# A two-layer streaming encoder on one core: the attention's order on VectorE, ScalarE and TensorE, and who scales the identity

## The chip, the cores and the metric

The kernel runs on one core of one Trainium2 chip. The metric is the device time of one execution in microseconds (us). A core has a matrix engine (TensorE, PE in the profile, with its weight loads as PEld), VectorE (DVE), ScalarE (ACT), GpSimd (POOL) and a queue engine that starts transfers (SyncE, SP). Each engine takes its instructions strictly in the order in which the program has them. They meet at semaphores alone.

## The reference

Two layers over 576 tokens (512 of a prompt in chunks of 64, 64 of a sample with 512 past ones), in fp32:

```
h = x + 1/2 SwiGLU_1(rms(x))
a = rms(h) @ w_in                     # split into three groups of heads
  A  latent attention, 6 heads: scores over the whole past, softmax, values from a 128-wide latent
  B  banded attention, 6 heads: 3 chunks of keys, a learned sink, a bias of slope * distance
  C  gated linear recurrence, 4 heads, then RMSNorm(o) * silu(g)
h = h + concat(A, B, C) @ w_out
h = h + 1/2 SwiGLU_2(rms(h))
h = h + sigmoid(rms(h) @ ple_gate) * (p @ ple_proj)
```

## The kernel before

It is written by hand: every engine has its own program, and the order of its lines is the order of the work. A loop runs over the two layers. In a layer the dense products (`dense`) take each weight tile as a high and a low half, three products each; before and after the attention they keep TensorE full. Between the last of them in `mixer_inputs` (`swq2`) and the first of the output projection (`out0`) stands `attention`, with no dense work beside it. This case is about that stretch.

**Units.** `attention` goes through 30 units: 6 pairs of heads times 5 variants v. v = 0 to 3 are the four blocks of 128 prompt queries, v = 4 is the sample. Pairs 0 to 2 (units 0 to 14) are the banded ones ("swa"): 128, 256, 256, 256 and 192 keys. Pairs 3 to 5 (units 15 to 29) are the latent ones ("mla"): 128, 256, 384, 512 and 576 keys. Before each latent pair `project` makes its keys, queries and values in six pieces, R, K, N, E, C, V.

**One unit through the engines.** TensorE makes the scores (`scores`) in one of two score slots in PSUM. VectorE adds the bias and the sink in banded units, takes the row maximum and scales it (`bound`). ScalarE takes the exponential and its row sum (`softmax_exp`). VectorE inverts the sum (`invert`). GpSimd multiplies the identity matrix by it (`scale_identity`, `scaled_id`). TensorE turns the probabilities with this scaled identity (`turn`), into one PSUM area (banks 6 and 7), so `turn` of a unit waits until ScalarE has copied the one before (`copy_t`). Then `weigh` multiplies by the values, into banks 4 and 5.

**The order before**, in iteration u, is: TensorE `scores(u+3)`, `turn(u+1)`, `weigh(u)` (turn first where a projection or the mean squares follow). ScalarE `copy_t(u+1)`, `softmax_exp(u+3)`. VectorE `invert(u+2)`, `bound(u+3)`. When a pair is through, `outputs` splits its 576 columns into `hid_hi` (ScalarE) and `hid_lo` (VectorE), and `weigh` of the next pair's unit with v = 0 waits for that, since it writes the same banks.

**The recurrence's tail** is worked off inside the attention: `head_out` copies its last result (`H1`), a Square makes `tmp`, `mean_squares` sums it on TensorE at u = `MEAN_SQUARES`, ScalarE takes a Sqrt, and `head_norm` on VectorE runs, behind `bound`, two reciprocals of 128x576, a scaling, a product and a subtraction at the units in `HEAD_NORM` and at `HEAD_HI` + 1. `take` copies the last level of the recurrence (`L13`), and `H1` on TensorE waits for it.

Of the kernel before, what the change touches and what calls it, by code (L numbers as in the profile page):

```python
# [23 lines left out]
F32 = mybir.dt.float32  # L24
# [6 lines left out]
P = 128  # L31
# [99 lines left out]
MEAN_SQUARES, HEAD_NORM, HEAD_HI = 8, (15, 16, 18, 19), 21  # L131
# [65 lines left out]
def hybrid_step(nc, x_t, p_t, w_all, uq, ukv, par_d, logits_d, cos_sin, ident_d, ones_d, head_ones_d, comb_d,  # L197
# [3 lines left out]
    with ctx:  # L201
# [68 lines left out]
        tmp = place("tmp", [P, 2, TOK], at=hid_at)  # L270
# [48 lines left out]
        def hg_bank(name):  # L319

            return 4 + 2 * (STEPS.index(name) % 2)
# [87 lines left out]
        att_hi = ev("att_hi", PAIRS)  # L409
        att_lo = ev("att_lo", PAIRS)  # L410
# [9 lines left out]

        out_flat = ps[:, 4:6, :].rearrange("p a n -> p (a n)")[:, 0:TOK]
# [95 lines left out]
        def _(act):  # L517
# [80 lines left out]
            def mixer_inputs(L):  # L598
# [37 lines left out]
                head_out(L, 1)  # L636
                act.wait_ge(O_out.sem, O_out.at(L, 4))
                act.activation(tmp[:, 0:2, :], hk[:, :, :], ACT.Square).then_inc(O_sq.sem, 1)
# [88 lines left out]
            def outputs(L, pair):  # L727

                act.wait_ge(pv_done.sem, pv_done.at(L, VARIANTS * (pair + 1)))
                if pair == 3:  # L730
                    act.wait_ge(O_norm.sem, O_norm.at(L, 3))
                act.activation(hid_hi[:, out_tile(pair), :], out_flat, ACT.Copy).then_inc(att_hi.sem, 1)

            def attention(L):
                softmax_exp(L, 0)
                softmax_exp(L, 1)
                copy_t(L, 0)
                softmax_exp(L, 2)
                for u in range(UNITS):
                    if u and u % VARIANTS == 0:  # L740
                        outputs(L, u // VARIANTS - 1)
# [15 lines left out]
                outputs(L, PAIRS - 1)  # L757
# [29 lines left out]
        def _(dve):  # L787
# [159 lines left out]
            def mixer_inputs(L):  # L947
                for name in W_IN:
# [42 lines left out]
                    elif name == "swk":  # L991
# [12 lines left out]
                        for j in range(2):  # L1004
                            dve.scalar_tensor_tensor(cq[:, j, :], cq[:, j, :],
                                                     par[:, PAR["q_norm"] + j:PAR["q_norm"] + j + 1],
                                                     c_root[:, :], ALU.mult, ALU.mult).then_inc(c_norm.sem, 1)
                    else:
                        scaled(L, u, halves(swq[:, int(name[3]), :])).then_inc(drained.sem, 1)
                dve.tensor_scalar(sink8[:, :], par[:, PAR["sink"]:PAR["sink"] + 6], 1 / SWA_SCALE, None, ALU.mult) \  # L1010
                   .then_inc(c_norm.sem, 1)
                take(L, 2 * LEVELS - 1)
# [125 lines left out]

            def bound(L, u):

                kind, pr, v = unit(u)
                b, x, nk = u % 2, X["s", u], unit_keys(u)
                made_wait(dve, L, x)
                if kind == "swa":
                    for a in range(2):
                        rows = slice(64 * a, 64 * a + 64) if v == 4 else slice(0, P)
                        at = 0 if v == 4 else a
                        hd = pr + 3 * a
                        if v == 4:
                            k0 = 64 * a  # L1150
                            dve.tensor_copy(score[rows, b, 0, nk:nk + 1], sink8[rows, hd:hd + 1])
                        else:
                            k0 = 128 if v == 0 else 0
                            if a == 0:
                                dve.tensor_copy(score[:, b, :, nk], sink8[:, pr:6:3])
                        slope = 2.0 ** (-8.0 * (hd + 1) / 6)
                        dve.scalar_tensor_tensor(score[rows, b, at, 0:nk], dist[rows, k0:k0 + nk],
                                                 -slope / SWA_SCALE, s_pair(x)[rows, a, 0:nk],
                                                 ALU.mult, ALU.add).then_inc(s_free[x % 2].sem, 1)
                    slot_wait(dve, L, x)  # L1160
                    n, src = (1, score[:, b, 0, 0:nk + 1]) if v == 4 else (2, score[:, b, :, 0:nk + 1])
                elif v == 4:
                    n, src = 1, s_flat(x)[:, 0:nk]
                else:
                    n, src = 2, s_pair(x)[:, :, 0:nk]
# [5 lines left out]
            def invert(L, u):  # L1171
# [5 lines left out]
                dve.reciprocal(stat[:, b, 6:6 + n], stat[:, b, 4:4 + n]).then_inc(recip_done.sem, 1)  # L1177

            def outputs(L, pair):

                dve.wait_ge(att_hi.sem, att_hi.at(L, pair + 1))
                dve.tensor_tensor(hid_lo[:, out_tile(pair), :], out_flat,
                                  hid_hi[:, out_tile(pair), :].bitcast(F32), ALU.subtract).then_inc(att_lo.sem, 1)

            def attention(L):
                dve.wait_ge(c_norm.sem, c_norm.at(L, 5))
                bound(L, 0)
                bound(L, 1)
                invert(L, 0)
                invert(L, 1)  # L1190
# [11 lines left out]
                outputs(L, PAIRS - 1)  # L1202
# [51 lines left out]
        def _(pool):  # L1254
# [37 lines left out]
            with pool.Fori(0, DEPTH) as L:  # L1292
# [17 lines left out]
                for u in range(UNITS):  # L1310
# [8 lines left out]
        def _(pe):  # L1319
# [291 lines left out]
            def turn(L, u):  # L1611
# [3 lines left out]
                if u == 0:  # L1615
# [257 lines left out]
```

## Time and profile before

| | us |
|---|---|
| median of 3 runs (2555.94 to 2561.65) | 2558.96 |
| the profiled execution | 2559.2 |
| its span | 2557.4 |
| attention of layer 1, 600.19 to 737.73 | 137.54 |
| attention of layer 2, 1856.77 to 1994.07 | 137.30 |

In the profile, "idle before" is the time in which the engine waited just ahead of an instruction, with the engine and line that ended it. PEclk is the share of full speed that TensorE was granted: 1.0 is 2.4 GHz, 0.5 is 1.2 GHz. A timeline row merges equal instructions ("x8").

### The profile page before, as it was taken

The page shows a single profiled execution, that of the slowest core. Times are in us where ns is not written, and L with a number is a line of the kernel's source. Part 1 is how long each engine was busy: PE and PEld are TensorE (multiplying, and loading weights), DVE is VectorE, ACT ScalarE, POOL GpSimd, SP SyncE. Part 2 cuts the span into 40 slices and gives each one's busy share as a digit, 9 for nine tenths or more (in the row PEclk, how much of TensorE's full clock was granted, in tenths as well). Part 3 has the DMA queues.
Part 4 walks back from the last instruction along what each step waited for, and adds up shares of the span by engine and source line. Part 5 has one row for each costly group of instructions (what it writes and reads, how often), then busy time and mean ns, then how long its engine had stood idle before and what let it go on. Part 6 is the DMA issues. An engine that isn't in the chain of part 4 may idle for free. (4 is left out here: it accounts for less than half of the span.)

```text
span 2557.4 us, 48070 instructions
## 1 busy us (share of the span) xinstructions
PE 2459.9 (96%) x19186; PEld 2384.1 (93%) x19186; DVE 1233.3 (48%) x1613; ACT 773.0 (30%) x1111; POOL 297.8 (12%) x211
## 2 busy tenths in 40 slices
PE   5999999998899999999999999999989999999996
PEld 5999999987689999999999999999857999999996
DVE  6434334775535434335654343458645354343466
ACT  3212223433543212223232221235245332221232
POOL 3000003101122000004300000040011400000043
PEclk9999999998999999999999999999989999999998
DMA  3322222211012222222223222232110222222222
GB/s 131 113 85 79 86 79 94 85 57 47 1 34 83 82 83 82 83 83 99 83 68 120 74 82 90 74 99 75 51 30 1 67 78 87 77 82 82 82 90 87
DMA packets 58569, 196.00 MB, mean 77 GB/s; under 512 B 8944, under 2 KB 11248, under 8 KB 58296
## 3 DMA queue, kind: packets, MB, share of 16 engines
q1 hardware_dynamic: 56848, 190.70, 22.7%
q10 hardware_dynamic: 1584, 3.37, 0.4%
q8 instruction: 98, 1.61, 0.3%
q14 instruction: 39, 0.32, 0.0%
HBM read 190.16 MB, written 3.88 MB: 76 GB/s over the span
## 5 line engine op out<-in xcount | busy, mean ns | idle before, releaser
L1343 PE MATMUL ps<-xg_hi,w_hi 128*128 128x288 f32 x3616 | 780.4, 297 | 32.4 <-DVE w_lo L796 28.3
L1343 PE MATMUL ps<-xg_lo,w_hi 128*128 128x288 f32 x3616 | 775.5, 296 | 0.0
L1343 PE MATMUL ps<-xg_hi,w_lo 128*128 128x288 f32 x3616 | 775.4, 296 | 0.0
L1343 PEld LDWEIGHTS ps<-xg_hi,w_hi 128*128 128x128 f32 x3616 | 584.2, 189 | 35.3 <-issue 28.3
L1343 PEld LDWEIGHTS ps<-xg_lo,w_hi 128*128 128x128 f32 x3616 | 584.2, 189 | 0.0
L1343 PEld LDWEIGHTS ps<-xg_hi,w_lo 128*128 128x128 f32 x3616 | 584.0, 189 | 0.0
L796 DVE TENSOR_TENSOR w_lo<-w_raw,w_hi 128x1024 fp32r<-128x1024 f32 x347 | 437.3, 1261 | 242.1 <-ACT w_hi L534 237.7
L534 ACT ACTIVATE w_hi<-w_raw 128x1024 fp32r<-128x1024 f32 x347 | 364.0, 1050 | 424.1 <-PE ps L1343 410.9
L1343 PE MATMUL ps<-hid_hi,w_hi 128*128 128x288 f32 x1664 | 356.6, 296 | 0.0
L1343 PE MATMUL ps<-hid_lo,w_hi 128*128 128x288 f32 x1664 | 356.2, 296 | 0.0
L1343 PE MATMUL ps<-hid_hi,w_lo 128*128 128x288 f32 x1664 | 356.2, 296 | 0.0
L1343 PEld LDWEIGHTS ps<-hid_hi,w_hi 128*128 128x128 f32 x1664 | 268.2, 189 | 0.1
L1343 PEld LDWEIGHTS ps<-hid_lo,w_hi 128*128 128x128 f32 x1664 | 268.2, 189 | 0.0
L1343 PEld LDWEIGHTS ps<-hid_hi,w_lo 128*128 128x128 f32 x1664 | 268.2, 189 | 0.0
L890 DVE SCALAR_TENSOR_TENSOR h<-ps,h 128x576 f32 (+1 forms) x96 | 72.7, 758 | 278.7 <-PE ps L1343 278.3
L575 ACT ACTIVATE hid_hi<-val 128x576 f32 (+1 forms) x88 | 60.3, 686 | 479.7 <-DVE val L871 479.7
L1258 POOL TENSOR_TENSOR acc<-h 128x576 f32<-128x576 f32 x9 | 12.0, 1333 | 1619.4 <-DVE h L890 1546.7
L816 DVE TENSOR_TENSOR val<-ps,r 128x576 f32<-128x576 f32 x88 | 66.6, 757 | 217.4 <-PE ps L1343 217.4
L816 DVE TENSOR_TENSOR gate<-ps,r 128x576 f32<-128x576 f32 x104 | 78.7, 757 | 174.0 <-PE ps L1343 172.4
L571 ACT ACTIVATE gate<-gate 128x576 f32<-128x576 f32 x88 | 60.4, 686 | 334.9 <-DVE gate L816 334.9
L1263 POOL TENSOR_TENSOR acc<-acc,sq 128x576 f32<-128x576 f32 x63 | 133.7, 2122 | 4.9
L1261 POOL TENSOR_TENSOR sq<-h 128x576 f32<-128x576 f32 x63 | 104.2, 1654 | 115.1 <-DVE h L1240 46.5
(208 smaller groups left out, 1669.8 us busy)
## 6 DMA issues: line engine op xcount, KB each, us to landing
w_raw<-w_all SPq DMA_DIRECT2D x347, 512.0 KB, 3.4
h<-x_t ACTq DMA_DIRECT2D x1, 2304.0 KB, 9.6
y_t<-y SPq DMA_DIRECT2D x8, 288.0 KB, 2.2
uq_w<-uq SPq DMA_DIRECT2D x2, 768.0 KB, 4.9
p_raw<-p_t SPq DMA_DIRECT2D x2, 576.0 KB, 7.0
ukv_w<-ukv SPq DMA_DIRECT2D x2, 384.0 KB
ckv<-ckv_c SPq DMA_DIRECT2D x2, 256.0 KB, 5.4
ckv_o<-ckv SPq DMA_DIRECT2D x2, 256.0 KB, 2.1
```

What stands on the lines that cost most here:

```text
L534: act.activation(w_hi[:, s, :], w_raw[:, n % RAW_SLOTS, :], ACT.Copy).then_inc(whi_ready.sem, 1)
L571: act.activation(gate[:, pr, :], gate[:, pr, :], ACT.Silu).then_inc(silu_done.sem, 1)
L575: act.activation(hid_hi[:, tile + pr + i * 2, :], val[:, pr, :], ACT.Copy) \
L796: dve.tensor_tensor(w_lo[:, s, :], w_raw[:, n % RAW_SLOTS, :], w_hi[:, s, :].bitcast(F32), ALU.subtract).then_inc(wlo_ready.sem, 1)
L816: return dve.tensor_tensor(out, slot(u), halves(r[:, :]), ALU.mult)
L890: dve.scalar_tensor_tensor(halves(h[:, m, :]), slot(v0 + q), 0.5, halves(h[:, m, :]), ALU.mult, ALU.add).then_inc(drained.sem, 1)
L1258: pool.tensor_tensor(acc[:, :], h[:, 0, :], h[:, 0, :], ALU.mult).then_inc(acc_done.sem, 1)
L1261: pool.tensor_tensor(sq[:, :], h[:, t, :], h[:, t, :], ALU.mult).then_inc(sq_done.sem, 1)
L1263: pool.tensor_tensor(acc[:, :], acc[:, :], sq[:, :], ALU.add).then_inc(acc_done.sem, 1)
L1343: ins = pe.matmul(ps[:, bank(u) + c, 0:HALF], w, m[:, k, c * HALF:(c + 1) * HALF], start=(k == kts[0] and i == 0), stop=(k == kts[-1] and ...
```

## The change

Six things change in one edit, all inside the attention or at its start.

1. VectorE's `bound` is cut in two. `bias` (sink and distance of a banded unit) goes ahead of `invert`, and `bound` keeps the maximum.
2. In latent units VectorE writes `scaled_id` itself, inside `invert`, ahead of the next maximum. GpSimd scales the identity in units 0 to 14 only.
3. `outputs` of a pair is in two parts, the 512 prompt columns and the 64 sample columns. `weigh` waits for part 0 at v = 0 and for part 1 at v = 4. On VectorE the parts stand behind `bound` of iterations 5p+5 and 5p+6 (p is the pair) where one subtraction stood ahead of `invert`.
4. ScalarE's last `head_out` goes behind the first two exponentials, and the Square behind that of unit 3. `H1` writes banks 4 and 5 where it wrote 6 and 7, so `weigh(0)` waits for `head_out` and `turn(0)` doesn't.
5. `take` of level 13 goes ahead of the weight split of the "spare" chunk, and the scaling of the sinks into `swk`'s work.
6. The mean squares move from u = 8 to 17, the two reciprocals from u = 15 and 16 to 18 and 19, the rest from 18, 19, 21 to 21, 22, 23, and `tmp` to another place in memory.

The constants, the bank of the recurrence's products, and ScalarE's `attention`:

```diff
-MEAN_SQUARES, HEAD_NORM, HEAD_HI = 8, (15, 16, 18, 19), 21
+MEAN_SQUARES, HEAD_NORM, HEAD_HI = 17, (18, 19, 21, 22), 23
...
-            return 4 + 2 * (STEPS.index(name) % 2)
+            return 6 - 2 * (STEPS.index(name) % 2)
...
             def attention(L):
                 softmax_exp(L, 0)
                 softmax_exp(L, 1)
                 copy_t(L, 0)
+                head_out(L, 1)
                 softmax_exp(L, 2)
                 for u in range(UNITS):
-                    if u and u % VARIANTS == 0:
-                        outputs(L, u // VARIANTS - 1)
...
+                    if u % VARIANTS == 4:
+                        outputs(L, u // VARIANTS, 0)
+                    if u and u % VARIANTS == 0:
+                        outputs(L, u // VARIANTS - 1, 1)
+                    if u == 0:
+                        act.wait_ge(O_out.sem, O_out.at(L, 4))
+                        act.activation(tmp[:, 0:2, :], hk[:, :, :], ACT.Square).then_inc(O_sq.sem, 1)
```

VectorE's `invert` (its last lines) and `attention`, then TensorE's `weigh`:

```diff
                 dve.reciprocal(stat[:, b, 6:6 + n], stat[:, b, 4:4 + n]).then_inc(recip_done.sem, 1)
+                if unit(u)[0] == "mla":
+                    dve.wait_ge(recip_done.sem, recip_done.at(L, u + 1))
+                    dve.wait_ge(id_ready.sem, id_ready.at(L, u))
+                    dve.wait_ge(turned.sem, turned.at(L, u - 1))
+                    for a in range(n):
+                        ins = dve.tensor_scalar(scaled_id[:, b, a, :], ident[:, :], stat[:, b, 6 + a:7 + a], None,
+                                                ALU.mult)
+                    ins.then_inc(id_ready.sem, 1)
...
                 for u in range(UNITS):
-                    if u and u % VARIANTS == 0:
-                        outputs(L, u // VARIANTS - 1)
                     if opens_mla_pair(u + 3):
                         project(L, unit(u + 3)[1])
+                    if u + 3 < UNITS and unit(u + 3)[0] == "swa":
+                        bias(L, u + 3)
                     if u + 2 < UNITS:
                         invert(L, u + 2)
                     if u + 3 < UNITS:
                         bound(L, u + 3)
+                    if u >= VARIANTS and u % VARIANTS in (0, 1):
+                        outputs(L, u // VARIANTS - 1, u % VARIANTS)
                     head_norm(L, u)
...
-                if v == 0 and u:
-
-                    pe.wait_ge(att_lo.sem, att_lo.at(L, u // VARIANTS))
+                if u == 0:
+                    pe.wait_ge(O_out.sem, O_out.at(L, 4))
+                if v in (0, 4) and u >= VARIANTS:
+
+                    pe.wait_ge(att_lo.sem, att_lo.at(L, 2 * (u // VARIANTS) - (1 if v == 0 else 0)))
```

First place: VectorE in a full banded unit. Before, iteration 0: `invert` (the reciprocal of `stat`), the sink's copy, the bias from `dist`, the maximum and its scaling.

```order
L428 REGISTER_ALU
L1177 RECIPROCAL stat_120<-stat_120 128x2
L1155 COPY score_85<-sink8_75 128x2
L1157 SCALAR_TENSOR_TENSOR score_85<-dist_66,ps 128x256 x2
L1166 TENSOR_REDUCE stat_120<-score_85 128x2
L1167 REGISTER_ALU
L1168 TENSOR_SCALAR stat_120<-stat_120 128x2
```

The changed kernel, the same iteration:

```order
L1158 COPY score_85<-sink8_75 128x2
L1160 SCALAR_TENSOR_TENSOR score_85<-dist_66,ps 128x256 x2
L429 REGISTER_ALU
L1186 RECIPROCAL stat_120<-stat_120 128x2
L1175 TENSOR_REDUCE stat_120<-score_85 128x2
L1176 REGISTER_ALU
L1177 TENSOR_SCALAR stat_120<-stat_120 128x2
```

The copy and the bias moved from behind the reciprocal, which waits for an exponential, to ahead of it.

Second place: VectorE around the two reciprocals of `tmp`. Before, they stand in iterations 15 and 16, and the next rows are piece R of the projection that iteration 17 opens.

```order
L1110 RECIPROCAL tmp_98<-tmp_98 128x576
L434 REGISTER_ALU
L1177 RECIPROCAL stat_120<-stat_120 128x2
L1166 TENSOR_REDUCE stat_120<-ps 128x1
L1167 REGISTER_ALU
L1168 TENSOR_SCALAR stat_120<-stat_120 128x1
L1110 RECIPROCAL tmp_98<-tmp_98 128x576
L438 REGISTER_ALU
L1128 TENSOR_TENSOR tq_99<-ps,cs_61 128x576
```

The changed kernel, from the maximum of unit 22 (iteration 19) to the subtraction of pair 3's prompt part (iteration 20):

```order
L1175 TENSOR_REDUCE stat_120<-ps 128x2
L1176 REGISTER_ALU
L1177 TENSOR_SCALAR stat_120<-stat_120 128x2
L1114 RECIPROCAL tmp_98<-tmp_98 128x576
L435 REGISTER_ALU
L1186 RECIPROCAL stat_120<-stat_120 128x2
L1192 TENSOR_SCALAR scaled_id_119<-ident_62,stat_120 128x128 x2
L1175 TENSOR_REDUCE stat_120<-ps 128x2
L1176 REGISTER_ALU
L1177 TENSOR_SCALAR stat_120<-stat_120 128x2
L1200 TENSOR_TENSOR hid_lo_53<-ps,hid_hi_52 128x512
```

The second reciprocal moved from in front of a projection to between two units of one pair, and the subtraction of the finished pair stands behind it and behind the maximum of unit 23.

Third place: ScalarE at the start of the attention. Before (`hk` is `head_out`, `tmp` the Square, `prob` the exponentials):

```order
L663 ACTIVATE hk_78<-ps 128x256
L663 ACTIVATE hk_78<-ps 128x320
L637 ISA
L638 ACTIVATE tmp_98<-hk_78 128x1152
L692 ISA
L699 ACTIVATE prob_117,stat_120<-score_85,stat_120 128x129 x2
```

The changed kernel:

```order
L697 ACTIVATE prob_117,stat_120<-score_85,stat_120 128x129 x2
L690 REGISTER_ALU
L697 ACTIVATE prob_117,stat_120<-score_85,stat_120 128x257 x2
L722 ACTIVATE probT_118<-ps 128x2x128
L661 ACTIVATE hk_78<-ps 128x256
L661 ACTIVATE hk_78<-ps 128x320
```

Two exponentials and a copy moved ahead of `head_out`; the Square moved further down.

## Rows read from the trace of the kernel before

**Rows 1.** The page: engines, busy time, share of the span, instructions.

```profile
PE 2459.9 (96%) x19186; PEld 2384.1 (93%) x19186; DVE 1233.3 (48%) x1613; ACT 773.0 (30%) x1111; POOL 297.8 (12%) x211
```

**Rows 2.** By stage: us, then busy us of PE, PEld, DVE, ACT, POOL, then PEclk.

```profile
600.19:654.42 54.23, 41.99 (x348) 30.53 (x349) 29.06 (x99) 27.76 (x79) 10.41 (x16) 0.81 0.12 36
654.42:737.73 83.31, 78.61 (x564) 59.97 (x562) 40.05 (x66) 42.03 (x100) 8.95 (x16) 0.98 0.00 1
1856.77:1912.43 55.66, 43.19 (x349) 31.96 (x349) 29.06 (x99) 27.99 (x79) 10.40 (x16) 0.79 0.12 35
```

**Rows 3.** TensorE and its granted clock (PEclk), in two short stretches.

```profile
632.00:636.00 4.00, 4.00 (x25) 0.57 0.00 0
...
680.00:684.00 4.00, 4.00 (x14) 0.57 0.00 0
...
1936.00:1940.00 4.00, 3.36 (x23) 1.00 0.02 4
```

**Rows 4.** Timeline of layer 1, start of attention (start, duration, engine, instruction, wait).

```profile
601.16 2.26 POOL L1307 COPY kT<-krs 32x1024 f32<-32x1024 f32 x2 [74.90 <-DVE swq L816]
...
601.31 1.96 DVE L796 TENSOR_TENSOR w_lo<-w_raw,w_hi 128x1024 fp32r<-128x1024 f32 x1 [0.33 <-ACT w_hi L534]
...
604.34 0.35 PE L1525 MATMUL ps<-A,V 64*64 64x64 f32 x5 [1.65 <-DVE A L1100]
...
609.57 1.16 ACT L638 ACTIVATE tmp<-hk 128x1152 f32<-128x1152 f32 x1
...
612.54 1.19 PE L1629 MATMUL ps<-scaled_id,prob 128*128 128x128 f32 x4 [2.60 <-POOL scaled_id L1284]
```

**Rows 5.** Timeline, one round of the banded units and the turn of unit 6.

```profile
615.53 0.17 DVE L1177 RECIPROCAL stat<-stat 128x2 f32<-128x2 f32 x1 [1.16 <-ACT prob L699]
...
616.44 0.69 DVE L1166 TENSOR_REDUCE stat<-score 128x2 f32<-128x514 f32 x1
...
618.53 0.17 DVE L1177 RECIPROCAL stat<-stat 128x2 f32<-128x2 f32 x1 [1.20 <-ACT prob L699]
...
627.13 1.13 PE L1629 MATMUL ps<-scaled_id,prob 128*128 128x128 f32 x8 [0.60 <-POOL scaled_id L1284]
```

**Rows 6.** Timeline, TensorE in front of `weigh` of unit 5.

```profile
630.54 0.44 PE L1653 MATMUL ps<-probT,swv 128*64 128x128 f32 x4 [2.28 <-DVE hid_lo L1182]
```

**Rows 7.** Timeline, the mean squares of unit 8 and the turn of unit 10.

```profile
638.95 1.28 ACT L748 ACT_TABLE_LOAD   x1 [0.78 <-PE ps L1538]
640.25 1.37 ACT L748 ACTIVATE tmp<-ps,eps 128x576 f32<-128x576 f32 x2
...
642.99 0.71 PE L1629 MATMUL ps<-scaled_id,prob 128*128 128x128 f32 x4
```

**Rows 8.** Timeline, the first long reciprocal, the turn of unit 18, then piece R.

```profile
674.02 3.75 DVE L1110 RECIPROCAL tmp<-tmp 128x576 f32<-128x576 f32 x1
...
678.63 2.49 PE L1629 MATMUL ps<-scaled_id,prob 128*128 128x128 f32 x16 [2.21 <-POOL scaled_id L1284]
...
680.92 3.35 PE L1558 MATMUL ps<-cq,uq_w 128*128 128x288 f32 x8
```

**Rows 9.** Timeline around unit 20: its exponential, turn of unit 21, `weigh` of unit 20.

```profile
692.94 0.37 ACT L705 ACTIVATE prob<-ps,stat 128x128 f32<-128x128 f32 x1
...
700.85 1.06 PE L1629 MATMUL ps<-scaled_id,prob 128*128 128x128 f32 x8
...
701.83 0.44 PE L1653 MATMUL ps<-probT,mv 128*64 128x128 f32 x4
```

**Rows 10.** VectorE groups by form: busy us, mean ns, idle before.

```profile
L1110 DVE RECIPROCAL tmp<-tmp 128x576 f32<-128x576 f32 x4 | 15.0, 3744 | 0.0
L1182 DVE TENSOR_TENSOR hid_lo<-ps,hid_hi 128x576 fp32r<-128x576 f32 x12 | 9.1, 757 | 28.2 <-ACT hid_hi L732 28.2
...
L1166 DVE TENSOR_REDUCE stat<-ps 128x2 f32<-128x1024 f32 x6 | 7.2, 1203 | 0.0
```

**Rows 11.** The page, the groups: the weight split of VectorE.

```profile
L796 DVE TENSOR_TENSOR w_lo<-w_raw,w_hi 128x1024 fp32r<-128x1024 f32 x347 | 437.3, 1261 | 242.1 <-ACT w_hi L534 237.7
```

More of the change, by code:

```diff
@@ L725, in copy_t, with outputs @@
                        .then_inc(probT_ready.sem, 1)
[L727 to L732, printed above, removed]
+            def outputs(L, pair, part):
+                cols = out_cols[part]
+                act.wait_ge(pv_done.sem, pv_done.at(L, VARIANTS * pair + 4 + part))
+                act.activation(hid_hi[:, out_tile(pair), cols], out_flat[:, cols], ACT.Copy).then_inc(att_hi.sem, 1)
             def attention(L):
@@ L1137, in project, with bias @@
                    .then_inc(s_free[dve_c % 2].sem, 1)
-            def bound(L, u):
-                kind, pr, v = unit(u)
+            def bias(L, u):
+                _, pr, v = unit(u)
                 b, x, nk = u % 2, X["s", u], unit_keys(u)
                 made_wait(dve, L, x)
-                if kind == "swa":
[L1145 to L1159, printed above, removed]
@@ new lines, in bias @@
+                for a in range(2):
+                    rows = slice(64 * a, 64 * a + 64) if v == 4 else slice(0, P)
+                    at = 0 if v == 4 else a
+                    hd = pr + 3 * a
+                    if v == 4:
+                        k0 = 64 * a
+                        dve.tensor_copy(score[rows, b, 0, nk:nk + 1], sink8[rows, hd:hd + 1])
+                    else:
+                        k0 = 128 if v == 0 else 0
+                        if a == 0:
+                            dve.tensor_copy(score[:, b, :, nk], sink8[:, pr:6:3])
+                    slope = 2.0 ** (-8.0 * (hd + 1) / 6)
+                    dve.scalar_tensor_tensor(score[rows, b, at, 0:nk], dist[rows, k0:k0 + nk],
+                                             -slope / SWA_SCALE, s_pair(x)[rows, a, 0:nk],
+                                             ALU.mult, ALU.add).then_inc(s_free[x % 2].sem, 1)
@@ L1177, in invert, with outputs @@
                 dve.reciprocal(stat[:, b, 6:6 + n], stat[:, b, 4:4 + n]).then_inc(recip_done.sem, 1)
[L1179 to L1183, printed above, removed]
+                if unit(u)[0] == "mla":
[6 more added lines that the diff above has]
+                    ins.then_inc(id_ready.sem, 1)
+            def outputs(L, pair, part):
+                cols = out_cols[part]
+                dve.wait_ge(att_hi.sem, att_hi.at(L, 2 * pair + part + 1))
+                dve.tensor_tensor(hid_lo[:, out_tile(pair), cols], out_flat[:, cols],
+                                  hid_hi[:, out_tile(pair), cols].bitcast(F32), ALU.subtract) \
+                   .then_inc(att_lo.sem, 1)
             def attention(L):
                 dve.wait_ge(c_norm.sem, c_norm.at(L, 5))
-                bound(L, 0)
-                bound(L, 1)
+                for u in range(2):
+                    bias(L, u)
+                    bound(L, u)
                 invert(L, 0)
+                bias(L, 2)
                 invert(L, 1)
@@ L1309, in _ @@
                         .then_inc(k_placed.sem, 1)
-                for u in range(UNITS):
+                for u in range(UNITS // 2):
                     scale_identity(L, u)
```

39 lines of the change are left out of this document (20 added, 19 removed).

## The prediction

> **What bounds the kernel now.** The page comes first: TensorE is busy for 96% of the span [rows 1], so only its idle time and the time at half clock can be won. The busy table by stage says where they are. The attention of layer 1 takes 137.5 us. In its banded part TensorE works 42.0 of 54.2 us at a mean clock of 0.81, in its latent part 78.6 of 83.3 us at 0.98; in layer 2 the banded part takes 55.7 [rows 2]. So the banded part is bound by waiting, with 12 us idle in each layer, and the latent part by TensorE itself: there each new wait of TensorE is lost in full. The dense stages are not touched. The timeline then says what TensorE waits for, and I follow it unit by unit. "T(u)", "S(u)" and "W(u)" are TensorE's `turn`, `scores` and `weigh` of unit u.
>
> **The gain in the banded part.** I shift the landmarks T(0), T(6), T(10) and the first projection, in layer 1.
>
> *The start.* T(0) runs at 612.54. It waits for an identity whose exponential stands behind `head_out` and a Square of 1.16 us, and `H1` itself waited 1.65 us for `take` behind a weight split of 1.96 us [rows 4]. Changed, `take` runs first and the exponential right after its maximum. VectorE still works off the split, two biases and two maxima, which ended near 607 before; the first reciprocal comes then, and GpSimd's identity 0.9 us later. T(0) at about 608.3, gain 4.2.
>
> *The round.* VectorE and ScalarE alternate: reciprocal at 615.53, next one at 618.53, 3.0 us a unit. From the first reciprocal to the maximum at 616.44 lie 0.91 us, and some 0.83 of them are copy and bias, which now run while ScalarE is at the previous exponential; the round falls to about 2.15 us. TensorE's own work for a full unit is a turn of 1.13 [rows 5], scores of about 0.6 and `weigh` of about 0.6, 2.3 us in all. So a full unit costs about 2.3, not 3.0. In pair 0 this is used up: `head_out` (0.7) and the Square (1.16) now stand among its exponentials. T(6), at 627.13, comes at about 623.35, gain 3.8.
>
> *The pair's end.* W(5) waited 2.28 us for `hid_lo` [rows 6]. In the new order W(5) waits for a subtraction behind `bound(8)`, which needs S(8), which TensorE issues only one turn ahead of W(5). From the end of S(8): bias 0.85, reciprocal and maximum with its scaling 1.1, subtraction 0.7, handovers 0.2, sum 2.85; TensorE has 1.1 of work. It idles about 1.75 us, so this part wins only 0.5 of each stop.
>
> *The mean squares leave.* At u = 8 they cost TensorE 2.1 us of products (8 of 288 columns, as piece R) and ScalarE a table load of 1.28 and 1.37 of Sqrt ahead of T(10) at 642.99, and the load stands again behind the Sqrt, for the next exponential [rows 7]. Without them a light unit is left there, about 2 us. T(10) at 633.85, gain 9.1, 4.1 of it from the mean squares. Pair 2 is shorter by three rounds of 0.7: the projection starts at 643.2, against 654.42 [rows 2]. **Gain 11.2 us**, and 12.6 in layer 2, whose banded part is 1.4 longer now at the same work [rows 2].
>
> **The losses in the latent part.**
>
> *W(15).* Before, the subtraction stood ahead of `invert` and W(15) waited little. Now it stands behind `bound(18)`, whose maximum over 1024 columns takes 1.20 [rows 10], and VectorE has also scaled two identities in each round. No row shows such a scaling of 128 columns. It is bounded by an instruction of two columns, 0.17 [rows 5], and by the subtraction of 576 columns, 0.76 [rows 10], whose share for 128 would be 0.17 as well; I take 0.35 for two of them, with 0.35 to 1.5 as ends (the two ends are the two rows taken as they stand; 1.5 would add 3.5 us to the chain of W(20) below). From the end of S(18): 0.1 + 0.6 (reciprocal, identities) + 1.2 + 0.2 + 0.7 + 0.1 = 2.9, against a turn of 1.06. Loss 1.85.
>
> *T(18).* It waited 2.21 us, since a reciprocal of 3.75 us stood ahead of its own [rows 8]. That wait is gone, which pays for W(15) and the identities: T(18) stays at 678.6.
>
> *Mean squares.* They now stand behind T(18): 2.1 us on TensorE, then piece R needs a slot that the table load and the first Sqrt free, 1.2 later: loss 3.3. In layer 1 T(18) took 2.49 and R 3.35 at half clock (0.57 over that stretch); at full clock they would take about 2.0 and 2.1, as in layer 2, where the clock stayed at 1.0 [rows 3, 8]. That is 1.7 back in layer 1. Together with rounding, the end of R is 1.85 later in layer 1 and 3.5 in layer 2.
>
> *W(20), the largest term.* The exponential of unit 20 started at 692.94 [rows 9]; the table load to come back from Sqrt now stands ahead of it, 1.28, so 694.2. On VectorE, one after the other: `invert(20)` from 695.05, with identities 0.6, `bound(21)` 0.9, **reciprocal 3.74**, `invert(21)` 0.6, `bound(22)` 1.15 (between the 0.69 of 512 columns and the 1.20 of 1024), **reciprocal 3.74** [rows 5, 10], `invert(22)` 0.6, `bound(23)` 1.4, subtraction 0.7, handover 0.1. That is 13.5 from 695.05, so 708.5, and W(20) before was at 701.83, directly behind T(21) [rows 9]. TensorE has nothing else it may issue. Loss 6.7. Behind W(20) stand S(24), T(22), W(21) and T(23); they follow at their own pace.
>
> *W(25).* As W(15), with the last subtraction of `head_norm` ahead, twice as wide as the 0.76 row: W(25) can go 1.45 later than before. Loss 1.45.
>
> *The clock.* After T(18)'s wait the granted clock fell to 0.57 in the mean of 4 us in layer 1, between the levels of 1.2 and 2.4 GHz, and stayed at 1.0 after the same wait in layer 2 [rows 3, 8]. A low stretch under full load costs about 1.6. I count one behind W(20) and one more, 1.5, for the five shorter waits of 1.2 to 1.85 us in a layer.
>
> **The sum.** Layer 1: 11.2 - 1.85 - 6.7 - 1.45 - 1.6 - 1.5 = -1.9. Layer 2: 12.6 - 3.5 - 6.7 - 1.45 - 1.6 - 1.5 = -2.15. That is 4.0 us slower than 2559.2, the profiled execution, which lies 0.2 above the median of 2558.96: 2563.2. A gain of the first half is taken away by the second.
>
> **A rule beside a row.** The weight split at 601.31 took 1.96 us, against 1.26 in the mean of its kind [rows 11], while GpSimd copied `kT` from 601.16 to 603.42 [rows 4]. The Trainium skill, GPSIMD Engine Reference, section 1 (Specifications), says that GpSimd's way to SBUF is shared with VectorE and that VectorE instructions with two SBUF inputs contend with it; the split has two, and the trace agrees. By that rule `take` loses nothing by going first, and the split, moved behind it, shortens by the part that then lies behind GpSimd's copy, about 0.5 us a layer; by the row alone it stays at 1.96. The sum above keeps 1.96; by the rule it would be 1 us better, 2562.2.
>
> **The rivals.**
>
> *A, the forecast:* the two halves nearly cancel, within 5 us of before. 0.43.
>
> *B, slower:* each of the shorter waits brings the half clock, as the wait of 2.21 us in layer 1 did [rows 3, 8]. Three more low stretches a layer at 1.5, less where TensorE waits anyway, give 3 to 4.5 a layer: 2570 to 2572. Half of it already decides, from 2564.1 on. For it: the idle time gets new places in the latent part, where TensorE is 94% busy now. Against it: the waits are shorter than that one, and after the same wait in layer 2 the clock stayed. 0.39.
>
> *C, faster:* the start no longer has the two waits of 1.65 and 2.60 us [rows 4], and the clock doesn't fall there at all. In the banded part, whose mean was 0.81 [rows 2], most of the low clock lies there. Then pair 0 runs 1 to 1.5 us faster, and with no low stretch but that behind W(20) a layer gains 2.5 to 3 over the sum: 2557.7. It decides (2553.8) only if the W(20) chain is also 2 us shorter than I have it, or the banded rounds reach 2.15 us in place of 2.3 (11 of them, 1.6 us a layer). 0.18.
>
> *D, the bias ahead of `invert` brings nothing,* since it has to wait for S(u+3) and then holds `invert(u+2)`. For it: same queue, in order. Against it: TensorE issues S(u+3) a full turn ahead. At 0.83 for nine full units it would be 7.5 us in each layer, 2578. It is in B's chance, as less than 0.03.
>
> About 0.2% is what a measurement of this kernel can tell from no change, here 5.1 us. Faster 0.18, same 0.43, slower 0.39. The range, 2552 to 2572, takes in B to its upper end and C to about its middle; the forecast's own is 2554 to 2564.
>
> **What would show it.** In the changed profile: T(0) near 608.3; reciprocals of `stat` 2.2 to 2.5 us apart in full banded units; the banded part, 600.2 to the first piece R, near 43 us in place of 54.2; in front of `weigh` of unit 20 an idle time of 6 to 7 us on TensorE put down to `hid_lo`; two table loads around the second projection; the latent part near 96 us in place of 83.3. Wrong would make it: a W(20) that follows T(21) at once, or low clock in other places than I have put it.

## The result and the profile after

The changed kernel takes 2555.52 us in the median of 20 runs (2551.26 to 2560.58), the one before 2559.58 in as many beside it. The medians lie 4.1 us apart. The ratio of the two sets is 0.9986, with an interval from 0.9980 to 0.9993, which is 3.6 us faster (1.8 to 5.1), where 4.2 slower was forecast. The gain is real and about as small as this measurement can tell. The profiled span is 2553.8 against 2557.4.

The busy table by stage of the changed kernel (us; busy of PE, PEld, DVE, ACT, POOL; PEclk; DMA share; GB/s): banded and latent part of layer 1, then of layer 2.

```profile
599.97:640.22 40.25, 33.40 (x342) 24.66 (x341) 27.73 (x100) 23.50 (x77) 9.41 (x16) 0.96 0.17 48
640.22:735.13 94.91, 81.83 (x573) 61.85 (x571) 47.08 (x97) 46.67 (x108) 0.40 (x1) 0.96 0.00 1
1853.68:1895.45 41.77, 34.90 (x341) 25.99 (x341) 27.73 (x100) 23.43 (x77) 9.41 (x16) 0.92 0.16 46
1895.45:1990.44 94.99, 82.21 (x572) 62.14 (x571) 47.08 (x97) 46.66 (x108) 0.40 (x1) 0.95 0.00 1
```

Against [rows 2] the banded part lost 14.0 and 13.9 us (forecast 11.2 and 12.6), and the latent part became 11.6 and 13.3 longer (forecast 13.1 and 14.75). So layer 1 is 2.4 faster and layer 2 0.5; the other 0.7 of the span is small shifts outside the attention. The forecast was right that two large amounts nearly cancel, and wrong about which is larger.

Timeline of the start of layer 1, where [rows 4] stood: GpSimd's copy, the split, `H1`, and the turn of unit 0.

```profile
600.95 1.26 POOL L1331 COPY kT<-krs 32x1024 f32<-32x1024 f32 x2 [74.94 <-DVE swq L819]
...
602.54 1.21 DVE L799 TENSOR_TENSOR w_lo<-w_raw,w_hi 128x1024 fp32r<-128x1024 f32 x1
...
602.79 0.35 PE L1549 MATMUL ps<-A,V 64*64 64x64 f32 x5 [0.32 <-DVE A L1104]
...
607.47 0.68 PE L1651 MATMUL ps<-scaled_id,prob 128*128 128x128 f32 x4 [1.17 <-POOL scaled_id L1308]
```

T(0) comes at 607.47 (forecast 608.3). The split takes 1.21 in place of 1.96 and GpSimd's copy 1.26 in place of 2.26: they no longer lie side by side, and the split is as short as the mean of its kind [rows 11]. T(0)'s four matmuls end in 0.68 us, not 1.19, since the clock is up. The next view is TensorE's granted clock over the first 20 us of the attention, layer 1 and 2, first of the kernel before and then of the changed one.

```profile
600.18:620.18 20.00, 15.45 (x159) 0.66 0.31 95
1856.77:1876.77 20.00, 15.46 (x159) 0.66 0.33 95
```

```profile
599.97:619.97 20.00, 17.10 (x213) 1.00 0.33 96
1853.68:1873.68 20.00, 17.10 (x213) 1.00 0.33 96
```

In the same time TensorE does 213 matmuls in place of 159. Further on in layer 1 the timeline has W(5), W(10) and the first piece R. [rows 6] had 2.28 us of waiting at W(5). Behind W(10) the clock still falls (0.66 in the mean of 635 to 640 us):

```profile
623.03 0.44 PE L1677 MATMUL ps<-probT,swv 128*64 128x128 f32 x4 [1.71 <-DVE hid_lo L1200]
...
635.15 0.44 PE L1677 MATMUL ps<-probT,swv 128*64 128x128 f32 x4 [1.71 <-DVE hid_lo L1200]
...
640.22 2.11 PE L1582 MATMUL ps<-cq,uq_w 128*128 128x288 f32 x8
```

And the latent part, layer 1: W(15), the table load and R(1), then the chain ahead of W(20), and W(25).

```profile
660.21 0.44 PE L1677 MATMUL ps<-probT,mv 128*64 128x128 f32 x4 [1.71 <-DVE hid_lo L1200]
...
667.22 1.28 ACT L744 ACT_TABLE_LOAD   x1
...
669.31 2.21 PE L1582 MATMUL ps<-cq,uq_w 128*128 128x288 f32 x8 [1.23 <-ACT tmp L744]
...
683.73 3.75 DVE L1114 RECIPROCAL tmp<-tmp 128x576 f32<-128x576 f32 x1
...
687.54 0.48 DVE L1192 TENSOR_SCALAR scaled_id<-ident,stat 128x128 f32<-128x128 f32 x2
...
689.00 3.75 DVE L1114 RECIPROCAL tmp<-tmp 128x576 f32<-128x576 f32 x1
...
693.20 1.22 DVE L1175 TENSOR_REDUCE stat<-ps 128x2 f32<-128x1024 f32 x1
...
694.53 0.68 DVE L1200 TENSOR_TENSOR hid_lo<-ps,hid_hi 128x512 fp32r<-128x512 f32 x1
...
695.36 0.69 PE L1677 MATMUL ps<-probT,mv 128*64 128x128 f32 x4 [6.06 <-DVE hid_lo L1200]
...
724.63 0.44 PE L1677 MATMUL ps<-probT,mv 128*64 128x128 f32 x4 [1.31 <-DVE hid_lo L1200]
```

Every stop of the forecast is there: 1.71 at W(15) (1.84 from its chain), 1.23 at R(1) (1.2), 6.06 at W(20) (6.7), 1.31 at W(25) (1.45). W(20)'s four matmuls take 0.69 in place of 0.44, since the clock is at half around the long stop (0.50 in the mean of 693.8 to 700.5 us).

### The profile page after: what moved, and what is told of

The parts are those of the page before. It is cut to its first block and busy times, and to the rows that moved or that the text cites. A ratio compares the mean times of both kernels' runs of the same rounds, so it can differ in the third digit from the quotient of the medians.

```text
span 2553.8 us, 48090 instructions
## 1 busy us (share of the span) xinstructions
PE 2450.7 (96%) x19186; PEld 2376.8 (93%) x19186; DVE 1244.0 (49%) x1679; ACT 772.3 (30%) x1123; POOL 278.7 (11%) x181
```

## The experiments

All twelve are edits of the changed kernel. Medians, and ratios to the kernel before on the same chip; stages in us, layer 1 / layer 2, from the one profiled execution. Kernels from different chips are compared by the ratio.

| kernel | median | ratio | span | banded | latent |
|---|---|---|---|---|---|
| before | 2559.58 | | 2557.4 | 54.2 / 55.7 | 83.3 / 81.6 |
| changed | 2555.52 | 0.9986 (0.9980 to 0.9993) | 2553.8 | 40.2 / 41.8 | 94.9 / 95.0 |
| E1 second reciprocal later | 2554.11 | 0.9981 (0.9971 to 0.9990) | 2548.5 | 40.2 / 41.8 | 91.9 / 92.5 |
| E2 GpSimd scales all | 2554.36 | 0.9976 (0.9966 to 0.9985) | 2548.6 | 40.2 / 41.8 | 92.1 / 92.4 |
| E3 bias behind `invert` | 2575.06 | 1.0062 (1.0045 to 1.0079) | 2573.6 | 49.2 / 49.2 | 95.0 / 95.0 |
| E4 old start | 2567.78 | 1.0032 (1.0018 to 1.0046) | 2562.0 | 44.0 / 46.6 | 94.8 / 94.6 |
| E5 `outputs` ahead, latent | 2547.93 | 0.9948 (0.9932 to 0.9965) | 2546.5 | 40.2 / 40.4 | 90.6 / 90.1 |
| E6 = E1 + E2 | 2546.96 | 0.9945 (0.9928 to 0.9961) | 2548.4 | 41.7 / 41.8 | 90.0 / 90.9 |
| E7 = E1 + E2 + E5 | 2536.82 | 0.9912 (0.9896 to 0.9929) | 2529.4 | 40.2 / 39.1 | 85.0 / 85.0 |
| E8 mean squares at 8 | 2552.15 | 0.9973 (0.9962 to 0.9983) | 2552.4 | 44.8 / 45.1 | 90.2 / 89.8 |
| E9 = E7, `outputs` first everywhere | 2539.60 | 0.9927 (0.9910 to 0.9943) | 2536.3 | 42.2 / 44.0 | 85.0 / 85.0 |
| E10 = E9 + E8 | 2541.41 | 0.9931 (0.9914 to 0.9948) | 2538.7 | 48.4 / 46.7 | 80.6 / 80.6 |
| E11 = E7 + E8 | 2537.51 | 0.9918 (0.9902 to 0.9935) | 2530.9 | 43.6 / 43.6 | 80.6 / 80.6 |
| E12 = E7 again | 2537.75 | 0.9908 (0.9888 to 0.9928) | 2538.7 | 41.8 / 41.8 | 85.0 / 85.0 |

**E1, the second long reciprocal leaves W(20)'s chain.**

```diff
-MEAN_SQUARES, HEAD_NORM, HEAD_HI = 17, (18, 19, 21, 22), 23
+MEAN_SQUARES, HEAD_NORM, HEAD_HI = 17, (18, 21, 22, 23), 24
```

> The changed kernel with the second long reciprocal behind the maximum of unit 24 (iteration 21, in front of the third projection) in place of iteration 19, and the three steps after it one iteration later. Theory A (the wait of 6.06 us in front of weigh of unit 20 is the two reciprocals in one chain): that wait falls by 3.7 to about 2.3 us, the low clock behind it gets shorter or goes, the latent part falls from 94.9 to about 90 us in each layer, the span from 2553.8 to 2543 to 2547. Rival B (VectorE is simply full in the latent part, and wherever the reciprocal stands something waits for it): the wait appears in front of piece R of the third projection or a turn behind it, and the span stays within 2 us of 2553.8.

Its timeline ahead of W(20), layer 1:

```profile
690.17 0.57 ACT L703 ACTIVATE prob<-ps,stat 128x384 f32<-128x384 f32 x1
...
690.86 0.17 DVE L1186 RECIPROCAL stat<-stat 128x2 f32<-128x2 f32 x1 [1.30 <-ACT prob L703]
...
693.62 0.44 PE L1677 MATMUL ps<-probT,mv 128*64 128x128 f32 x4 [3.85 <-DVE hid_lo L1200]
```

The stop falls by 2.2 (expected 3.7), and no new one appears; the latent parts are 3.0 and 2.5 shorter (expected 4.9), and the span stays 1.5 above the expected 2543 to 2547. The reciprocal was worth 2.2 of its 3.75, mainly because once it is gone `invert(22)` waits 1.30 for the exponential of unit 22. That wait my expected 2.3 us had left out. The second reciprocal is a cause of the stop, but only down to the next arrival. What is shown is the length of the stop. In total time neither E1 nor E2 or E8 is told from the changed kernel: their intervals overlap with 0.9980 to 0.9993. The spans of E1 and E2, 5.3 and 5.2 below the changed kernel's, are each from the third shortest of ten executions.

**E2, who scales the identity.** VectorE's scaling in `invert` is taken out, and GpSimd's loop runs over `range(UNITS)` in place of `range(UNITS // 2)`.

> The changed kernel with GpSimd scaling the identity in all 30 units, as before. Theory A (in the latent part TensorE waits for VectorE's chain, and VectorE's own scaling lengthens it by 0.4 to 0.5 us a unit): the waits in front of weigh of units 15, 20 and 25 fall by 0.4, 1.3 and 0.4 us, the span falls by 2 to 4 us, to about 2551. Rival B (the turn waits for the scaled identity, so VectorE's shorter way to it, about 0.35 us, is what pays): turns of latent units wait for GpSimd and the span rises by 2 to 6 us. Rival C: neither is waited for, within 1 us.

W(15) waits 1.31 (from 1.71), W(20) 4.62 (from 6.06), W(25) 1.31 as before, and no turn waits for GpSimd. The 1.44 of W(20) is three pairs of scalings at the 0.48 that the rows above show, one in each `invert` of its chain. Letting VectorE scale the identity made the stops longer and shortened no other wait of the latent part.

**E3, the bias behind `invert` again.**

```diff
-                    if u + 3 < UNITS and unit(u + 3)[0] == "swa":
-                        bias(L, u + 3)
                     if u + 2 < UNITS:
                         invert(L, u + 2)
+                    if u + 3 < UNITS and unit(u + 3)[0] == "swa":
+                        bias(L, u + 3)
```

Ahead of the loop `bias(L, 2)` goes behind `invert(L, 1)` in the same way.

> The changed kernel with bias put back behind invert, so that a banded unit's bias waits for the exponential again. Theory A (the round of VectorE and ScalarE sets the pace of the banded part, and the 0.83 us of the bias is on it): full banded units go from about 2.3 to 3.0 us, the banded part grows by 5 to 7 us in each layer, the span to 2564 to 2568. Rival D (TensorE's own work sets the pace anyway): below 2 us a layer, span under 2558.

The banded part of layer 1, then W(5) in it:

```profile
603.05:652.30 49.25, 36.68 (x340) 26.98 (x341) 28.47 (x100) 23.77 (x77) 9.41 (x16) 0.86 0.14 39
```

```profile
629.89 0.69 PE L1677 MATMUL ps<-probT,swv 128*64 128x128 f32 x4 [3.42 <-DVE hid_lo L1200]
```

The banded parts grow by 9.0 and 7.4, more than the 5 to 7 expected. Of that 5.7 in either layer is idle time of TensorE (49.25 - 36.68 = 12.57 against 6.85, and 12.57 against 6.87), the rest low clock. W(5) and W(10) stop exactly twice as long, 3.42, and the turns wait up to 1.43. So the new place of the bias is the main step of the change. Another 3.1 of the 19.8 in the span come before the attention, where the edit touches nothing: low clock at the first matmuls and behind a wait near 538 us (below, E12).

**E4, the old start:** `head_out` and the Square ahead of the first exponentials, `take` of level 13 behind the split.

> The changed kernel with the start as before: the last head_out and the Square ahead of ScalarE's first exponentials, take of level 13 behind the weight split. Theory A (the waits at the start both cost their own length and bring the low clock from about 605 to 618, which costs more): the first turn comes 4 to 5 us later, the granted clock is at half for some 13 us again, the banded part grows by 5 to 7 us in each layer, the span to 2564 to 2568. Rival (the clock there doesn't follow the waits): the clock stays at 1.0 after 605 and a layer loses 2 to 4 us, because the Square leaves the rounds of pair 0, span 2558 to 2562.

The turn of unit 0 in layer 1 and in layer 2:

```profile
610.90 0.68 PE L1649 MATMUL ps<-scaled_id,prob 128*128 128x128 f32 x4 [3.12 <-POOL scaled_id L1306]
```

```profile
1870.07 1.19 PE L1649 MATMUL ps<-scaled_id,prob 128*128 128x128 f32 x4 [2.60 <-POOL scaled_id L1306]
```

The banded parts grow by 3.8 and 4.8, less than the 5 to 7 expected, and the span of 2562.0 lies at the rival's upper end; the rival's clock of 1.0 did not come. Over their first 20 us the clock is 0.91 in layer 1, where it falls just behind T(0), and 0.66 in layer 2, as before the change. In the changed kernel and in the eleven edits that keep its start, 24 stages in all, that mean is 1.00 each time. The low clock belongs to the old start.

**E5, the subtraction ahead of `invert`,** for u from 15 on; **E6,** E1 and E2 together; **E7,** all three.

```diff
+                    if u >= 15 and u % VARIANTS in (0, 1):
+                        outputs(L, u // VARIANTS - 1, u % VARIANTS)
                     if u + 2 < UNITS:
                         invert(L, u + 2)
...
-                    if u >= VARIANTS and u % VARIANTS in (0, 1):
+                    if VARIANTS <= u < 15 and u % VARIANTS in (0, 1):
```

> The changed kernel, but in the latent units (u from 15 on) VectorE's two `outputs` parts of a finished pair stand ahead of `invert` again, as before the change; the banded units stay as changed. Theory A: of the latent stops, W(15) 1.71, W(20) 6.06 and W(25) 1.31 us, the part that is spent in queue behind `invert` and `bound` comes back. W(15) and W(25) fall to under 0.5, W(20) loses an `invert` (0.6) and a `bound` (1.4) of its chain and goes to about 4.0; some 0.7 is given back where `invert` stands behind the subtraction. Span 2546 to 2549, against 2553.8 of the changed kernel. Rival: the subtraction delays the next identity by 0.7 each time and the stop moves to the turn behind it; the latent part keeps its 94.9 us and the span is 2552 to 2556.

> Both earlier edits at once: the second long reciprocal of `tmp` in iteration 21 in place of 19 (the rest at 22, 23, 24), and GpSimd scales the identity in all 30 units. Alone each took 5.3 and 5.2 us off the span of the changed kernel, 3.0 and 2.8 us of the latent part of layer 1. Theory A: both shorten the same chain in front of W(20), one after the other: W(20) idles 3.85 - 1.44 = 2.4 us, W(15) 1.31, W(25) 1.31, latent part near 89.1, span 2543 to 2545. Rival: another chain (exponential of 23 behind the table load) already stands behind the 3.85, so W(20) stays at 3.5 or more and the span at 2546 to 2549.

> The two edits on the reciprocals and on GpSimd, and in the latent units the `outputs` parts ahead of `invert`. Theory A: what VectorE queues in front of `hid_lo` is all there is in the latent stops, so all three are nearly gone: W(15) and W(25) under 0.5, W(20) about 1, latent part near 86.5 in place of 94.9 us, span 2537 to 2541, median about 2543. Rival: the turns now wait for GpSimd behind the subtraction, latent part 88.5 or more, span 2543 or more.

W(20) in E5, E6 and E7, layer 1:

```profile
695.53 0.69 PE L1679 MATMUL ps<-probT,mv 128*64 128x128 f32 x4 [4.14 <-DVE hid_lo L1200]
```

```profile
695.27 0.44 PE L1669 MATMUL ps<-probT,mv 128*64 128x128 f32 x4 [2.41 <-DVE hid_lo L1192]
```

```profile
689.16 0.44 PE L1671 MATMUL ps<-probT,mv 128*64 128x128 f32 x4 [1.51 <-DVE hid_lo L1192]
```

E5: W(15) and W(25) have no wait over 0.3 any more, W(20) loses 1.9 (expected 2.0); 0.85 comes back at T(18) and 0.60 at T(28). E6: 2.41, to the hundredth what the two effects add up to (3.85 - 1.44). Its span stayed 3.4 above the top of the expected range, with 2.6 before the attention and 1.4 in a banded part whose clock is 0.92. E7: a latent part of 85.0, against 94.9 in the changed kernel and 86.5 expected, with W(15) and W(25) no longer waiting and W(20) at 1.51 (about 1 expected); the median is 2536.8, about 6 us below the expected 2543. Its stage rows, layer 1 banded and latent, layer 2 banded and latent:

```profile
600.00:640.25 40.25, 33.39 (x342) 24.74 (x341) 27.73 (x100) 23.50 (x77) 9.41 (x16) 0.96 0.16 48
640.25:725.22 84.97, 79.20 (x573) 60.16 (x571) 40.39 (x70) 46.82 (x108) 8.94 (x16) 1.00 0.00 1
1842.07:1881.17 39.10, 31.87 (x341) 23.55 (x341) 27.74 (x100) 23.57 (x77) 9.41 (x16) 1.00 0.17 49
1881.17:1966.13 84.96, 79.20 (x573) 60.16 (x571) 40.38 (x70) 46.81 (x108) 8.95 (x16) 1.00 0.01 1
```

Three of the four stages run at full clock, so 31.87 and 79.20 are TensorE's busy time in them with no low clock at all. That gives a scale for every other row with as many matmuls.

**E8, the mean squares back at u = 8** (`MEAN_SQUARES` alone).

> The changed kernel with the mean squares back at u = 8; the reciprocals and the rest of `head_norm` stay in their new places. It prices moving them. The forecast had 4.1 us a layer as the gain in the banded part, 3.3 as the loss before R(1) (2.0 of it the products), and 1.28 of the loss at W(20), the table load ahead of the exponential of unit 20. If it is right: banded part 40.25 + 4.1 = 44.3, W(20) idle 6.06 - 1.28 = 4.8, latent part 94.9 - 4.6 = 90.3, span 2553 within 1.5. Rival: in the banded part the products fill time in which TensorE waits anyway. Undoing the bias order cost 9.0 and the start 3.8 of the 14.0 us that layer 1 won, which leaves 1.2 for them; then the banded part is 41.5 and the span 2547 within 1.5.

Banded 44.8 and 45.1 (expected 44.3), latent 90.2 and 89.8 (90.3), W(20) 4.89 (4.8), span 2552.4 (2553): the forecast's price of the mean squares holds in each place, and the rival is out. Moving them gave 4.5 and 3.3 and took 4.7 and 5.2: nothing, or a small loss that the medians can't tell.

**E9, the subtraction first in the banded units too** (ahead of `bias`); **E10,** E9 with the mean squares at 8; **E11,** E7 with them at 8.

> The kernel with all three edits (late reciprocals, GpSimd scales all identities, subtractions ahead of `invert` in latent units), and now VectorE's subtraction stands first in its iteration in banded units too, ahead of `bias`. Theory A: the stops at W(5) and W(10), 1.71 us in every run so far, are queue time on VectorE behind `bias`, `invert` and `bound` of the next unit, as the forecast had them (2.85 us of chain against 1.1 of work). ScalarE's half is done by then, so both go to under 0.4 and about 0.4 of each comes back at the turn behind: banded part 37.5 to 38.5 in place of 40.25, median 5 us below the 2536.8 of the kernel with three edits, 2531 within 3. Rival: TensorE would have to wait anyway, for the exponential of unit 7 or 12 and its identity, which the subtraction now holds up; the stop moves to T(7), the banded part stays at 39.5 or more and the median at 2535 to 2539.

> The same with the mean squares back at u = 8. In the changed kernel that cost 4.5 and 3.3 us in the two banded parts and gave back 4.7 and 5.2 in the latent parts, 1.4 of the span in all. Theory A: the products and the wait ahead of R(1), 3.3 us, come back again, and of W(20)'s 1.5 us 1.3 at most; in the banded part they cost at least the 4.5 as no stop at W(10) is left to share: equal to the kernel without this edit within 2 us. Rival: the banded part with its stops gone is bound by ScalarE (two table loads and two Sqrt, 5.3 us), and it costs 6 or more: 3 us or more slower than that kernel.

> All three edits, mean squares back at u = 8. With the subtractions first in all units the same step gave back 4.4 us in each latent part (84.97 to 80.58) and took more than 4.5 in the banded part where that had its own stops. Theory: banded part 44.8 and latent part 80.6, sum equal to the kernel without the step (125.2) within 1 us; median within 2 us of its 2536.8. Rival: without the mean squares' wait ahead of R(1) the clock holds there too, and the step is a gain of 2 us or more.

Timeline of E9 around W(5), with the turns of units 7 and 8:

```profile
621.89 0.57 ACT L729 ACTIVATE hid_hi<-ps 128x512 fp32r<-128x512 f32 x1
...
622.50 0.69 DVE L1192 TENSOR_TENSOR hid_lo<-ps,hid_hi 128x512 fp32r<-128x512 f32 x1 [1.64 <-ACT hid_hi L729]
...
623.34 0.44 PE L1669 MATMUL ps<-probT,swv 128*64 128x128 f32 x4 [1.30 <-DVE hid_lo L1192]
...
624.83 1.13 PE L1643 MATMUL ps<-scaled_id,prob 128*128 128x128 f32 x8 [0.58 <-POOL scaled_id L1300]
...
628.24 1.13 PE L1643 MATMUL ps<-scaled_id,prob 128*128 128x128 f32 x8 [1.27 <-POOL scaled_id L1300]
```

Theory A falls. VectorE stands 1.64 at the subtraction, waiting for ScalarE's half, which comes behind the exponential; W(5) still waits 1.30, and the bias, `invert` and maximum queued behind come late, 1.27 at T(8). In the banded parts TensorE is idle for 10.2 and 9.0 us (E7: 6.9 and 7.2), so there the changed kernel's place for the subtraction is the better one; the medians of E9 and E7, from two chips, are too close to say it. In the latent units the old place is the better one (E5), though VectorE waits there even longer. This is its subtraction ahead of W(15) in E7:

```profile
657.74 0.69 DVE L1192 TENSOR_TENSOR hid_lo<-ps,hid_hi 128x512 fp32r<-128x512 f32 x1 [1.79 <-ACT hid_hi L729]
```

The instructions behind it are held up in the same way, but T(18) then waits only 0.49. A likely reason, not tested, is that TensorE has more work there: turns of the latent units 19 to 21 start 3.6 and 3.2 us apart in E7, those of the banded units 7 to 9 2.1 and 2.3.

E10 is 1.8 slower than E9 in the median, which the intervals can't tell from nothing, so its theory A stands for the total: the banded parts are 6.2 and 2.6 longer, the latent parts 4.4 shorter each. E11 and E12 are equal (2537.51 and 2537.75, on one chip): the latent part is 4.4 shorter, the banded part 4.5 longer at equal clock (34.31 busy of 43.57 in the row below, against 31.87 of 39.10 in E7).

```profile
1843.44:1887.01 43.57, 34.31 (x350) 25.00 (x350) 27.69 (x100) 27.52 (x81) 9.43 (x16) 1.00 0.15 44
```

**E12, E7 again,** on another chip.

> The kernel with all three edits once more, on another chip, since its profiled execution (span 2529.4) was the fastest of its four (2531.2 to 2539.8) and showed no low clock in three of its four attention stretches. The latent parts had no wait over 1.51 us. Theory: the stops are fixed by the program and repeat to 0.05 us (W(20) 1.51, W(5) and W(10) 1.71), while the clock behind them does not; median 2534 to 2540, latent parts 85 us if the clock holds, 86 to 87 if it falls once. Rival: the latent part without a low clock was luck, and it comes out at 87 or more in both layers.

The stops ahead of W(5), W(10) and W(20) repeat to 0.01 us and the latent parts to 0.02; the median is 2537.75. The span of the profiled execution is 9.3 longer, nearly all of it slower matmuls: 2.8 ahead of the attention of layer 1, 2.2 between the two attentions, 1.5 and 2.7 in the banded parts. Of the 2.8, 1.1 is there from the start: 0.3 is a later first matmul, and 0.8 comes because the first dense matmuls take 0.68 us a pair, in place of 0.42, until 33.4 us and not until 31.2. Here are 535 to 545 us, ahead of the attention, in E7 and in E12.

```profile
535.00:545.00 10.00, 8.22 (x100) 1.00 0.01 2
```

```profile
535.00:545.00 10.00, 7.97 (x76) 0.83 0.00 0
```

The wait in this stretch is the same (1.08 and 1.09 us, then 0.65 in both), but in E12 the matmuls behind it run at half clock for a while, and the dense ones go on at 545.61 and not 542.90: 2.7 later, 1.1 of it old, 1.6 from here. (The counts, 100 and 76, hold both.) E3, E5 and E6 have this low stretch as well, for 1.6 to 1.7 us each; the rest of the 2.6 to 3.1 by which their attention starts later than the changed kernel's is there from the first matmuls.

## Why the prediction was wrong, step by step

**What failed is the term "Gain 11.2 us"** (12.6 in layer 2) of the banded part, which was 14.0 and 13.9, and in it the step "In pair 0 this is used up", which put the gain at T(6) at 3.8 where it was 6.9. The losses of the latent part, 1.5 and 1.4 too large, add to it. The two are 4.1 and 2.9 of the 7.6 us between forecast and measured span. The forecast had 4.05 slower, so with the banded gain alone put right it would have been no change. The measured 2555.52 lies in the stated range of 2552 to 2572 and less than 5 us from before, as A had it, but on the other side of before. The landmarks of layer 1:

| | forecast | measured |
|---|---|---|
| T(0) | 608.3 | 607.47 |
| T(0) to T(6) | 15.05 | 12.72 |
| T(6) to T(10) | 10.5 | 9.94 |
| T(10) to R(0) | 9.35 | 10.09 |

The largest error is pair 0. Three things are in it. I took rounds of 2.3 us from durations added up; from reciprocal to reciprocal, where no stop lies between, they are 2.0 to 2.2, since turn, scores and `weigh` overlap at their ends. I charged `head_out` and the Square at 0.7 and 1.16 among the exponentials; TensorE waited 0.47 and 0.57 there. And I measured the gain from a start whose half clock I did not price: with the old start back, the clock of the first 20 us is 0.91 and 0.66 again, and TensorE is busy 1.7 and 3.2 us longer in the banded parts (E4).

The other way to read the 14.0 us is by the full-clock scale of E7 and E11. Before, TensorE was busy for 41.99 [rows 2]; as many matmuls at full clock take 34.31 (E11), so 7.7 was low clock. Changed, 33.40 against 31.87 leaves 1.5. The gain is 6.2 of clock, 2.4 of mean squares and 5.4 of idle time. In layer 2 the clock gives 5.9 (8.9 less 3.0). The forecast saw the mean of 0.81 [rows 2] and still had no gain of clock in its banded part. This was rival C's mechanism, which I held at 0.18; its own condition, that the rounds reach 2.15, came true.

**Right:** T(0)'s reason; the bias ahead of `invert` as the main gain (E3); the pair's end, 1.71 for "about 1.75"; the price of the mean squares (E8); W(20) as the largest loss. Its chain took 13.05 where I had 13.5. An identity pair costs VectorE 0.48 (I took 0.35, inside the bounds of 0.35 to 1.5).

**The latent losses** were 11.6 and 13.3 for 13.1 and 14.75. Every term was somewhat too large: the end of R came 1.5 and 3.1 later (1.85 and 3.5), W(20) 6.3 later than R (6.7), and what stands behind it took 3.9 and 4.0 (4.55: W(25) and the clock). The sum for R had an error of its own: 3.3 less 1.7 is 1.6, and the 0.25 that the forecast calls rounding has no row. In layer 1 idle time is 8.4 of the 11.6 (13.08 against 4.70 in [rows 2]) and busy time 3.2, of which the mean squares are 2.1 and low clock 1.1; the forecast had a net 1.4 of clock there (1.6 and 1.5 lost, 1.7 back). In layer 2 low clock is 3.0, for 3.1. So the size of the clock's loss was right, and its place only in part: it fell around W(20) in both layers, where it costs 2.6 and 3.0 and I had 1.6, and at no other stop of the latent part.

**Rival B** is out: of the five short stops of a layer none in the latent part was followed by a low clock; in the banded part W(10) was in both layers, W(5) in layer 2 alone, 1.5 us each. Before the change both stops were already followed by one, in both layers, so no place is new. **Rival D** is out by E3.

**The split.** The row of before gave 1.96, and the sum kept it; it took 1.21, and GpSimd's copy lost 1.0 as well. The Trainium skill, GPSIMD Engine Reference, section 1 (Specifications), says that VectorE instructions with two SBUF inputs contend with GpSimd. These two rows agree, and the effect was larger than the 0.5 us that I read from the rule. E4 is the test of it: with the old start the split lies beside the copy again, and both have their old lengths, 1.96 and 2.26, where all kernels with the new start have 1.21 or 1.22 for the split.

```profile
601.26 2.26 POOL L1329 COPY kT<-krs 32x1024 f32<-32x1024 f32 x2 [74.97 <-DVE swq L818]
601.41 1.96 DVE L798 TENSOR_TENSOR w_lo<-w_raw,w_hi 128x1024 fp32r<-128x1024 f32 x1 [0.33 <-ACT w_hi L535]
```

That 0.75 is nearly all of the error at T(0).

**Not additive.** Undone alone, start, bias and mean squares cost 3.8, 9.0 and 4.5 in layer 1, 17.3 together, against 14.0 for the change as a whole. The overlap is in the waits: the three bring back 10.0 of idle time (2.1, 5.7 and 2.2), where the change as a whole took out 5.4. The products are 2.4 either way, and low clock is 4.9 (1.7, 3.3 and nothing) against 6.2. A reading that fits, not tested by itself: in the kernel before a slow TensorE covered part of what would otherwise have been waiting.

**Open:** why the same wait is followed by a low clock in one execution and not in another. No run here settles it. What the old start does to the clock is shown; which of its two waits does it was not taken apart. Before the change the clock was at half from 605 us on (0.50 in the mean of 605 to 609), ahead of the wait of T(0), so there the wait of `H1` was enough; in layer 1 of E4 it was still 1.00 in that stretch. What cutting `outputs` in two parts brought (W(5) waits 1.71 and not 2.28), and what the new place of the first long reciprocal brought, no run takes apart.

## What to carry to other kernels

Where TensorE's mean clock in a stretch is well below 1, put a price on its recovery as well as on the waits: a change that takes the waits out there can get both. Ask of every instruction that is to go ahead of a wait whether its own input is already there. The bias's was. The subtraction's was not: put first, it waited 1.64 us (E9) and 1.79 (E7) for ScalarE and held up all behind it. Then ask who needs what is held up: in the banded units TensorE did, in the latent units it seems to have had other work for most of that time. When a stop stands behind several queued items, their prices add exactly until another arrival takes over (3.75 us of reciprocal were worth 2.2). The best kernel here is E7: it keeps the new order of the banded units, gives the scaling back to GpSimd and puts the subtraction ahead of `invert` again in the latent ones, and moves the second reciprocal further back: 0.9912 of before (E11, with the mean squares at 8, is equal to it).

## What was not expected of the hardware

The stops of `weigh` of one program repeat between two chips to 0.01 us (E7, E12), while the granted clock behind them does not, and one low stretch of the kind in E12 costs about 1.6 us. The length of a stop doesn't say whether it comes. These are 6 us from W(5) on in the changed kernel, layer 1 and layer 2, each behind a wait of 1.71 us:

```profile
623.03:629.03 6.00, 6.00 (x56) 1.00 0.00 0
1876.75:1882.75 6.00, 6.00 (x44) 0.72 0.00 0
```

The Trainium skill, TensorE: Matmul & The Clock Gate, Part 1, says that the number of slow matmuls at the start of one kernel differs from run to run. E7 and E12 agree: their first dense matmuls are slow until 31.2 us in one and until 33.4 in the other. There it is read from the durations; the granted clock of the profile shows 1.00 in both (28 to 36 us).
